# Prompt attention of a hybrid decoder step: from blocks of 16 queries over all heads in the latent space to one head at a time with decompressed keys and values

## The reference

```
q_nope, q_rope = q[..., :64], rope(q[..., 64:], pos)          # 8 heads, 64 + 32
q_lat = einsum('bthn,rhn->bthr', q_nope, w_ukv[..., :64])     # into the latent space, rank 128
s = (einsum('bqhr,bkr->bhqk', q_lat, c_kv) + einsum('bqhe,bke->bhqk', q_rope, k_rope)) * SCALE
p = softmax(where(k <= q, s, -inf))                           # prompt: causal over 528 rows
o_lat = einsum('bhqk,bkr->bqhr', p, c_kv)
o_mla = einsum('bthr,rhv->bthv', o_lat, w_ukv[..., 64:])
```

## Time and profile before

| | us |
|---|---|
| median of 3 runs | 2067.08 (2061.88 to 2074.32) |
| the profiled execution, its own time | 2087.52 |
| its span, first to last instruction | 2085.6 |
| TensorE busy | 1713.7 |
| VectorE busy | 743.8 |
| ScalarE busy | 409.5 |

### The profile page before, as it was taken

How to read it: one execution, slowest core, us unless ns; L and a number is a source line. 1 busy time by engine, 2 the same in 40 slices (tenths; PEclk the granted TensorE clock), 3 DMA queues, 4 the chain that set the end, 5 groups by cost and what they waited for, 6 DMA issues and landing times. The chain is left out here.

```text
span 2085.6 us, 20855 instructions
## 1 busy us (share of the span) xinstructions
PE 1713.7 (82%) x8111; PEld 1155.8 (55%) x8111; DVE 743.8 (36%) x1492; ACT 409.5 (20%) x883; POOL 120.7 (6%) x132
## 2 busy tenths in 40 slices
PE   4999967998889747999199998789998996399960
PEld 3767645656767643444176765466676776144430
DVE  2724635443311231222453273443423013222216
ACT  2221132122210201222132110411222012022210
POOL 1000001001100021000110000000000000300001
PEclk9989857579979858999698996855989895699985
DMA  8211354001205016998441109410111411299954
GB/s 243 63 33 39 22 31 76 0 1 54 99 1 161 1 47 205 322 343 279 155 67 41 41 21 28 38 51 0 51 51 51 150 32 46 92 307 337 329 175 149
DMA packets 234209, 220.71 MB, mean 106 GB/s; under 512 B 91818, under 2 KB 207863, under 8 KB 231927
## 3 DMA queue, kind: packets, MB, share of 16 engines
q1 hardware_dynamic: 217526, 153.96, 30.3%
q0 software_dynamic: 11824, 48.01, 6.5%
q10 hardware_dynamic: 4752, 17.30, 2.1%
HBM read 187.36 MB, written 31.85 MB: 105 GB/s over the span
## 5 line engine op out<-in xcount | busy, mean ns | idle before, releaser
L423 PE MATMUL ps<-const,over 128*128 128x128 f32 (+6 forms) x980 | 167.9, 301 | 134.9 <-DMA over<-x_rows,fetch 60.2
L965 ACT ACTIVATE over<-ps 128x512 f32<-128x512 f32 (+7 forms) x348 | 163.4, 504 | 540.6 <-PE ps L466 152.7
L466 PE MATMUL ps<-xT,wslot 128*128 128x296 f32 x960 | 254.6, 424 | 5.2 <-SPq L376 4.1
L861 PE MATMUL ps<-over 128*128 128x512 f32 x512 | 234.1, 611 | 22.9 <-DMA over<-in_moe_w_up 21.3
L423 PEld LDWEIGHTS ps<-const,over 128*128 128x128 f32 (+6 forms) x980 | 126.1, 155 | 184.5 <-DMA over<-x_rows,fetch 60.4
L466 PEld LDWEIGHTS ps<-xT,wslot 128*128 128x128 f32 x960 | 185.5, 196 | 63.9 <-issue 6.1
L861 PEld LDWEIGHTS ps<-over 128*128 128x128 f32 x512 | 97.2, 195 | 140.5 <-issue 113.3
L1275 DVE COPY over<-ps 128x128 f32<-128x128 f32 (+3 forms) x188 | 84.0, 462 | 145.2 <-PE ps L466 66.6
L813 PE MATMUL ps<-mix,wslot 128*128 128x296 f32 x512 | 128.1, 413 | 1.7 <-PEq L376 1.7
L1796 DVE TENSOR_SCALAR over<-over 128x256 f32<-128x256 f32 x33 | 9.7, 294 | 328.5 <-ACT over L1218 303.4
L877 PE MATMUL ps<-over 128*128 128x512 f32 x256 | 115.3, 593 | 1.2 <-DVE over L1275 1.2
(11 more groups left out here) (321 smaller groups left out, 2206.5 us busy)
## 6 DMA issues: line engine op xcount, KB each, us to landing
over<-in_moe_w_gate SPq DMA_DIRECT2D x33, 1024.0 KB, 9.7
over<-in_moe_w_up SPq DMA_DIRECT2D x33, 1024.0 KB, 12.1
over<-in_moe_w_down SPq DMA_DIRECT2D x33, 1024.0 KB, 5.9
y_rows<-over ACTq DMA_DIRECT2D x33, 512.0 KB, 7.1
wslot<-in_w_in SPq DMA_DIRECT2D x30, 512.0 KB, 4.0
wslot<-in_w_out SPq DMA_DIRECT2D x16, 512.0 KB, 4.3
y_rows<-over SPq DMA_DIRECT2D x1, 4608.0 KB, 16.4
x_rows<-zT SPq DMA_DIRECT2D x2, 2048.0 KB, 6.8
```

Of the source, the lines that this page charges most:

```text
L423: return nc.tensor.transpose(out, in_, ident[0:n, 0:n])
L466: i = mm(b[:, 0:HALF], wslot[:, u % NSLOT, k, :], xT[:, k, SH[h]], start=(k == 0), stop=(k == KD - 1))
L861: i = mm(b, xgT[:, e % 2, k, :], wgu[:, e % 2, k, :], start=(k == 0), stop=(k == KD - 1))
L965: rel(f_(dst, src, ACT.Copy), key, "A")
```

## The change

The prompt's attention goes head by head. Keys `kh` (64 decompressed + 32 rotated rows) and values `vh` are formed once per layer, queries `qh` are laid out per head. There are 10 units: two for the last 16 queries (4 heads each, in four 32-row strips), then 8 heads with their 512 queries in four blocks of 128, causal, so 10 blocks of 128x128 scores, all products 96 deep. Values of two heads are formed side by side in PSUM rows 0 to 63 and 64 to 127, straight into `mix`. The buffers of probabilities are 2, those of turned ones 3. In each step ScalarE takes the unit's exponentials first, then copies earlier values and turned probabilities.

The sample's parts change too: the two sequences' products alternate between the upper and lower 64 PSUM rows in `scores_of` and `latents_of`, where the turned probabilities become the weights and the gathered latents the moving side, so that the result is turned back (`latents_turned`). `qlat` and the last product through `wukv` cover the sample's 64 rows alone. The two barriers around the prompt's attention go, on all engines. The router's ranking takes 5 + 5 products in place of 15 + 5.

```
 # TensorE
-                for m in range(8):
+                for m in (4, 5, 6, 7, 0, 1, 2, 3):
                     for h in range(2):
                         b = group(("q", l, m, h), "A" if m < 6 else "D")
...
+                for j in range(4):
+                    for x in range(2):
+                        b = group(("kd", l, j, x), "DA"[x])
+                        done(mm(b[:, 0:KH], wukv[:, j * P:(j + 1) * P], ckv[:, x * KH:(x + 1) * KH], start=True, stop=True))
+                for t in range(NB + 1):
+                    n = P if t < NB else TP - NB * P
+                    b = group(("v", l, t), "DA"[t % 2])
+                    done(mm(b[0:n, :], ckv[:, t * P:t * P + n], wukv[:, 512:1024], start=True, stop=True))
...
+                drained(("kd", l, 3, 0))
+                drained(("kd", l, 3, 1))
+                wait("q_rotated", l + 1)
+                wait("keys_spread", l + 1)
...
+                    hd = u - 2
+                    for x, parts in enumerate(HEAD_SCORES):     # ((3,0),), ((2,0),(0,384)), ((1,0),)
+                        b = group(("s", l, u, x), "E")
+                        for qb, at_ in parts:
+                            w = (qb + 1) * P
+                            i = mm(b[:, at_:at_ + w], qh[0:96, hd, qb * P:(qb + 1) * P], kh[0:96, hd, 0:w], start=True, stop=True)
...
+                    for kb in range(NB):
+                        for a in range(2):
+                            hd = 2 * j + a
+                            i = mm(b[64 * a:64 * a + 64, kb * P:NB * P], vh[:, kb, hd * MV:(hd + 1) * MV],
+                                   pT[:, (u + a) % 3, pt_at(kb):pt_at(kb + 1)], start=(kb == 0), stop=(kb == NB - 1))
...
+                for step in range(NU + 1):
+                    if step < NU:
+                        scores(step)
+                    if step >= 3 and step % 2 == 1:
+                        values(step - 3)
+                    if 1 <= step <= NU:
+                        turned(step - 1)
...
-                            for jj in range(4):
+                        for jj in range(4):
+                            for s in range(2):
...
-                        for j in range(16):
-                            mm(o, kg[:, s, j * LAT:(j + 1) * LAT], psT[:, j * P + 64 * s:j * P + 64 * s + 64], start=(j == 0), stop=False)
+                    for j in range(16):
+                        for s in range(2):
+                            mm(b[64 * s:64 * s + 64, 0:LAT], psT[:, j * P + 64 * s:j * P + 64 * s + 64], kg[:, s, j * LAT:(j + 1) * LAT],
+                               start=(j == 0), stop=False)
...
-                for t in range(TT):
-                    o = b[:, t * E:(t + 1) * E]
-                    i = mm(o, cst("before"), r4[:, t, :], start=True, stop=(t == 0))
-                    for u in range(t):
-                        i = mm(o, ones, r4[:, u, :], start=False, stop=(u == t - 1))
+                mm(b[:, 0:TT * E], cst("before"), every, start=True, stop=False)
+                for d in range(1, TT):
+                    mm(b[:, d * E:TT * E], ones, every[:, 0:(TT - d) * E], start=False, stop=(d == TT - 1))
 # ScalarE
+                f_(kh[64:96, :, :], kro[0:ROPE, 0:TP].unsqueeze(1).to_broadcast([ROPE, H, TP]), ACT.Copy)
+                act.drain().then_inc(S("keys_spread"), 1)
+                for t in (1, 3):
+                    copy(("v", l, t), vh[:, t, :], bank(("v", l, t)))
...
+                            for qb, at_ in parts:
+                                w = (qb + 1) * P
+                                i = f_(pq[:, sl, p_at(qb):p_at(qb) + w], bank(key)[:, at_:at_ + w], ACT.Exp, bias=nmq[:, sl, qb:qb + 1],
+                                       scale=SCALE, accum_out=smq[:, sl, qb:qb + 1])
...
+                for step in range(NU + 1):
+                    if step < NU:
+                        exps(step)
+                    if step >= 3 and step % 2 == 1:
+                        values_out(step - 3)
+                    if 1 <= step:
+                        turned_out(step - 1)
 # VectorE
+                    for x, parts in enumerate(HEAD_SCORES):
+                        key = ("s", l, u, x)
+                        full(dve, key)
+                        for qb, at_ in parts:
+                            own = bank(key)[:, at_ + qb * P:at_ + (qb + 1) * P]
+                            stt(own, cst("before"), NEG, own, ALU.mult, ALU.add)
                         dve.drain()
+                        for qb, at_ in parts:
+                            v.tensor_reduce(mxq[:, sl, qb:qb + 1], bank(key)[:, at_:at_ + (qb + 1) * P], AX.X, ALU.max)
...
+                for step in range(NU + 1):
+                    if step >= 1:
+                        normed(step - 1)
+                    if step < NU:
+                        maxima(step)
+                    if step >= 1:
+                        turned_out(step - 1)
 # POOL
-                        barrier(pool, "pool")
+                        pool.wait_ge(filled, index[("s", l, NU - 1, 2)] + 1)
```

## The result

The changed kernel takes 1864.5 us (median of four runs, 1854.7 to 1872.0) against 2068.7 for the kernel before (2061.9 to 2074.3): a ratio of 0.901, 95% interval 0.896 to 0.906. The forecast was 1855, or 0.898. The profiled execution is the fastest of the four, 1854.7 us with a span of 1852.9, and the one of before lay 0.9% above its median; so the traces differ by 233 us and the medians by 204. Where the text reads windows and timelines, it compares these two traces.

A forecast was written before the change was run, and what follows sets the result against it. TensorE was taken to set the pace in both attentions, VectorE to end the first stage. Terms of -213.8 us took the profiled 2087.5 to 1873.7, by the runs' median 1855; forecast 1825 to 1890, range 1808 to 1925.

The forecast's parts named there:

- First stage, -5.5: Queries and latents before the attention: 31.7 us worked out against 37.5, taken as 5.5 us less a layer.
- Attention, -53.5: Prompt's attention: a chain over VectorE and ScalarE takes 7.5 us a head, stage 73.7 us against 127.3, each layer.
- rival 1: Clock stays at 1.2 GHz through attention and sample: 1986 us, chance 0.10; in the attention alone 1882, within the forecast.
- Sample, -42.1 and -45: Sample's attention, layers 0 and 1: overlapping halves of PSUM's rows and narrower latents save 42 and 45 us.
- Rivals 2 and 4: Sample: 2, halves don't overlap, 1950 us, chance 0.08; 4, each change of half empties the array, 2127, chance 0.03.
- Ranking, -4.4: Router's ranking: 20 records go, saving 4.4 us a layer, with VectorE and POOL waiting behind them.
- Rival 3, longer hand-overs: Prompt's attention: a head takes 10 us, +20 us a layer, 1895 us; chance 0.12.
- Rival 5, the order moves nothing: Prompt's attention: ScalarE's order of exponentials and copies moves nothing and shifts no number; likely true, 0.9.
- The sum: Whole kernel: first stage, attention and ranking in two layers plus both samples, -213.8 us from the profiled 2087.5.

The follow-up runs named there:

- e5: Changed kernel with each score product of the prompt's attention issued twice: attention +5.0 us a layer against 78.4, time up 12 us.
- e6: Changed kernel without VectorE's four causal masks a head: attention -9.3 us a layer, a head 5.86 us, time down 8 us.
- e11: Changed kernel with the causal masks added by TensorE in PSUM instead of by VectorE: attention 69.8 and 72.1 us, heads of 5.86.
- e3: Changed kernel with the sample's scores one sequence after the other instead of alternating: quarter 2.68 us, sample 17 us longer in each layer.
- e4: Changed kernel with the sample's latents one sequence after the other instead of alternating: 64 records 6.84 us against 3.74, sample longer by 13.6 and 12.1.
- e7: Changed kernel with the ranking's 15 products of one token tile each back: ranking to first up-projection +4.4 us in each layer, time up 18 us.
- e1: Changed kernel with ScalarE's copies ahead of its exponentials in each step: some 2 to 3 us a layer worse in the traces, same time intervals.
- e2: Changed kernel with VectorE taking a head's maxima before scaling the head before: 12 us slower, 7.2 to 9.9 us a head.
- e9: e2 plus TensorE's scores issued a step earlier, ahead of the turns: attention 92 us, no gain.
- e10: e9 plus VectorE's copy of turned probabilities given to ScalarE: attention 60.25 us in both layers, 1826.4 us, 2.0% under the changed kernel.
- e13: e10 with the scores back in their old place behind the turns: attention 89.7 and 89.2 us.
- e12: Edits of e10 and e11 together on the changed kernel: attention 64.7 and 66.0 us, worse than e10 alone, as is the time.

## Why the prediction was right

The mechanism and its order of terms held, and the time forecast is 9 us below the measured 1864.5, inside the range. By its own steps, measured with the windows above:

- **First stage, -5.5.** -4.8. The terms add up to 31.7 us, which would be -5.8; layer 0 took 32.7: the spread of the rotated key 3.72 (forecast 3.8) and the copies 4.50 (1.4 + 1.1 + 3.2) were as good or better, but ScalarE's last copy of a query ended 19.5 us after the stage's start, not 18, and from the last copy to the first score 1.3 us passed, not 1. No experiment isolates this stage.
- **Attention, -53.5.** -54.1. Masks took 0.290 each, as taken from the nearer row; the links measure 3.30, 2.22 and 1.65, 7.17 in sum against 7.3 worked out and 7.5 taken, so no drain was left over to add. Units of the last queries and the tail were as forecast within a microsecond, but for one head of 8.8 us behind the values of the last 16 queries (rival 1). e5, e6 and e11 show the chain, and that TensorE hides beneath it.
- **Rival 1, low clock.** The clock does fall to 1.2 GHz in the attention, mostly for parts of a head, and such a head keeps its 7.17 us, since what the clock lengthens is hidden. Where it stayed low for 10 us on end it wasn't: from 366.90 to 376.90 TensorE was busy throughout at 0.50 (the window above), VectorE waited for the scores, and this head took 8.78 us, close to the 8.9 that the prediction gives for the low clock. In the sample the clock stayed at 2.4 but for the pause at the end.

```profile
373.46 4.14 PE L719 MATMUL ps<-over,zT 96*128 96x512 f32 x8
```

- **Sample, -42.1 and -45.** -49.1 and -53.4. Two terms were mis-sized and one is missing. The last pair's latents were put at 7.2 us, the low clock's price, and took 4.1 at 2.4 GHz (11.7 gained instead of 8.5). The turn back of three results was to cost 1.5 us and costs about 0.2. The missing term is the opening of layer 0's stage: its first scores ran at a low clock before (0.57, below), and from its start to its first latents 7.1 us are gone, of which four quarters explain 3.9. Quarters (2.70 to 1.73, 16 times: 15.5) and the end (9.6 to 3.0: 6.6) are as forecast, the other latents (8.12 to 4.04, three times: 12.2) 1 us less. Together 49. Layer 1 gave back the whole difference to layer 0, 4.1 us, where 3 were taken. Rivals 2 and 4 are out by e3 and e4: the halves overlap, and a change of half costs nothing that 1.73 us leaves room for.

```profile
486.00:490.00 4.00, 3.56 (x12) 2.09 (x13) 0.00 (x0) 0.30 (x1) 0.00 (x0) 0.57 0.71 293
```

- **Ranking, -4.4.** 4.3 us in the timeline above, 8.6 in e7's: -4.3.
- **Rival 3, longer hand-overs (10 us a head).** Out: 7.17.
- **Rival 5, the order moves nothing.** In the time, yes. In e1's trace the order moves 2 to 3 us a layer, 0.2 to 0.4 in three heads and the rest at the stage's end.
- **The sum.** Worked out -213.8; by the traces -233, of which the stages named here hold 231 in the two layers; by the medians -204. The two profiled runs lie at opposite ends of their runs, so the traces say more than the medians, and the ratio, 0.898 forecast and 0.901 measured, is the fair comparison. Where the 27 us between the two lie isn't shown, as the kernel before was traced once. That the forecast came within 10 us is luck in part: its terms fell 17 us short of the traced gain, and the scatter of the runs took more than that back.

What failed came after the prediction: the account of e2, that a swap in one list would break the chain, and of e9, that a second one would. The chain moved onto TensorE's list, and then onto one copy in VectorE's.

## What to carry to other kernels

When a stage is bound by a chain between engines, work added on a third engine costs little (e5) and work taken off the chain pays in full (e6, e11); two engines' brackets that name each other show it. To break such a chain, follow every list in which the next step's work stands behind this step's result, small copies too: the three edits of e10 gained 18 us a layer, and the parts of them that were run (e2, e9, e13) each lost 11 to 14; the scores ahead or ScalarE's copies without VectorE's swap weren't run. Once it is broken, the edit that paid before can cost (e12).

## What the runs showed of the hardware

- Products that write the two halves of PSUM's rows run fully at once when they alternate in TensorE's list (1.73 us for 20 records that take 2.68 with the sequences in two blocks), and hardly at all in long blocks (64 records: 0.107 us each and 6.84 us in two blocks, 3.74 alternating).
- Where TensorE's pauses were longer, its clock was lower: the attention's granted clock over the windows was 0.79 and 0.85 in the changed kernel's two layers, 0.89 in e10 and 0.71 in e13 (84.6 us, TensorE busy for 63.0), where pauses of 3 us stood ahead of the turns; at the end of e1's stage a pause of 5.47 us instead of 2.38 came with 0.50 instead of 1.00. A link on TensorE can so cost more than its length (ten turns 2.40 us instead of 1.31). That the pauses cause it is argued: busy stretches stood at the low clock too (0.50 from 366.90 to 376.90).
- A record of the ranking takes 0.23 us on average at a granted clock of 0.50, whether it moves 16 columns (2.29 for 10) or 16 to 64 (1.81 for 8): there dropping records paid (e7), and by these rows narrowing them from 64 columns wouldn't.
